# A hybrid decoder step on one core: the gate products of a mixture-of-experts expert run ahead of its up products, over four column groups, and expert 0's down products run behind expert 1's up products

## The reference, cut to what matters

```
def run_block(args):
    idx_b, e = args
    xb = xpad[idx_b]
    hb = jax.nn.silu(xb @ w_gate[e]) * (xb @ w_up[e])
    return hb @ w_down[e]
```

## Time and profile before

| | us |
|---|---|
| median of 3 runs | 1528.69 (1527.49 to 1530.44) |
| the profiled execution's own time | 1532.22 |
| its span, first to last instruction | 1530.1 |

### The profile page before, as it was taken

One profiled execution on the slowest core, in us unless ns is written; L12 is line 12 of the kernel. 1 busy time (PEld: TensorE's weight loads), 2 busy tenths in 40 slices (PEclk: granted clock), 3 DMA queues, 4 the chain that ended last, 5 costly groups with the idle time before them and its releaser, 6 DMA issues.

```text
span 1530.1 us, 19858 instructions
## 1 busy us (share of the span) xinstructions
PE 1325.7 (87%) x8056; PEld 764.3 (50%) x8056; DVE 531.9 (35%) x1086; ACT 263.2 (17%) x688; POOL 87.0 (6%) x251
## 2 busy tenths in 40 slices
PE   7999999999999999899778777867877876877786
PEld 6667777765579996354333333332332342342232
DVE  5287767332564445414003103102202202202234
ACT  4452232262231112030000000000000000000003
POOL 7800000010010002000000000000000000000000
PEclk9999999999999999888888988998987988987988
DMA  9332332361359845999999999999999999999997
GB/s 222 114 111 64 102 111 60 106 171 38 130 182 360 327 155 197 398 429 427 429 425 431 426 431 426 430 427 430 427 430 426 430 427 430 429 428 427 428 424 309
DMA packets 117111, 481.00 MB, mean 314 GB/s; under 512 B 17969, under 2 KB 85877, under 8 KB 90341
## 3 DMA queue, kind: packets, MB, share of 16 engines
q1 hardware_dynamic: 115432, 475.71, 78.0%
q0 software_dynamic: 1328, 4.37, 1.0%
q10 hardware_dynamic: 288, 0.04, 0.0%
HBM read 470.03 MB, written 10.78 MB: 314 GB/s over the span
## 4 chain that ended last, share of the span: by engine, by line
PE 54%; DMA 40%; DVE 2%; issue 1%; SPq 1%; ACT 1%; POOLq 0%; POOL 0%; ACTq 0%; DVEq 0%
DMA arena<-in_w_up 40%; PE ps L2290 20%; PE ps L2595 12%; PE ps L2343 7%; PE ps L2653 2%; PE ps L2360 2%; PE ps L2428 1%; PE ps L2225 1%; PE ps L2160 1%; PE ps L2148 1%; PE ps L2627 1%; SPq L585 1%; PE ps L2504 1%; DMA arena<-in_x_prompt 1%; PE ps L2212 1%
## 5 line engine op out<-in xcount | busy, mean ns | idle before, releaser
L2595 PE MATMUL ps<-arena 128*32 128x512 f32 x2048 | 294.1, 725 | 136.1 <-DMA arena<-in_w_up 134.7
L2290 PE MATMUL ps<-arena 128*128 128x336 f32 (+1 forms) x1152 | 328.3, 442 | 0.0
L2290 PEld LDWEIGHTS ps<-arena 128*128 128x128 f32 x1152 | 215.3, 190 | 95.9 <-issue 3.7
L2595 PEld LDWEIGHTS ps<-arena 128*32 128x32 f32 x2048 | 79.8, 129 | 323.5 <-issue 321.0
L2653 PE MATMUL ps<-arena 128*32 128x512 f32 x1024 | 147.6, 727 | 19.0 <-DVE arena L1924 18.3
L1912 DVE COPY arena<-ps 128x512 f32<-128x512 f32 x31 | 21.4, 692 | 406.6 <-PE ps L2595 406.5
L2428 PE MATMUL ps<-arena 128*128 128x128 f32 (+1 forms) x672 | 125.7, 318 | 0.0
L2428 PEld LDWEIGHTS ps<-arena 128*128 128x128 f32 (+1 forms) x672 | 95.3, 196 | 47.2 <-issue 24.9
L1232 ACT ACTIVATE arena<-ps 128x128 f32<-128x128 f32 x32 | 8.9, 277 | 625.0 <-PE ps L2627 624.9
L2343 PE MATMUL ps<-arena 128*128 128x128 f32 x896 | 106.0, 278 | 0.0
L2343 PEld LDWEIGHTS ps<-arena 128*128 128x128 f32 x896 | 101.8, 192 | 5.4 <-issue 4.8
(11 more groups left out here) (433 smaller groups left out, 1055.1 us busy)
## 6 DMA issues: line engine op xcount, KB each, us to landing
arena<-in_w_down SPq DMA_DIRECT2D x59, 2048.0 KB, 23.1
arena<-in_w_gate SPq DMA_DIRECT2D x57, 2048.0 KB, 19.0
arena<-in_w_up SPq DMA_DIRECT2D x57, 2048.0 KB, 23.4
arena<-in_w_in SPq DMA_DIRECT2D x15, 2048.0 KB, 9.2
arena<-in_w_out SPq DMA_DIRECT2D x8, 2048.0 KB, 9.9
arena<-in_w_gate SPq DMA_DIRECT2D x14, 1024.0 KB, 11.6
arena<-in_w_up SPq DMA_DIRECT2D x14, 1024.0 KB, 13.3
arena<-in_w_down SPq DMA_DIRECT2D x10, 1024.0 KB, 11.9
```

Source lines behind the costliest of these rows:

```text
L2290: mm = te.matmul(o, w, x, start=(k == 0), stop=(k == kt - 1))
L2595: mm = te.matmul(ps[CAP * x:CAP * x + CAP, 0, :], (xT0 if start else xt)[:, 4 * q + at, CAP * i:CAP * i + CAP], (next_second[up] if late a ...
```

## The change

It does four things.

1. An expert's pieces 0 to 3 are its gate weights and 4 to 7 its up weights. TensorE runs eight steps `s_` of one piece each: four of gate products, then four of up products, all over the four column groups.
2. The turn becomes two (`turn_half`): the gate half after step 3, the up half after step 7, each with its own DVE copy of the bank before it and 4 products against 32 columns of `fold`. Silu follows the gate half; the multiplication follows the up half.
3. A transfer of two pieces waits for two steps of the last expert, wherever it stands; the first six of expert 1 are single pieces. Expert 0's down products (`down(0, 0, False)`) stand behind expert 1's up products.
4. In expert 31 the parts of `add_back_third` stand ahead of steps 0, 2 and 4, and `take_rows` ahead of step 6 behind a wait for Silu. ACT takes Silu after the square of row group 1; DVE copies the gate sums between its fourth and fifth `add_part`.

The diff, cut to its core:

```diff
             sp.wait_ge(piece_loaded[3], 16)
-            sp.dma_start(next_second[1], A["w_up"][0, 1]...[:, 2048:4096])
+            sp.dma_start(next_second[1], A["w_gate"][0, 1]...[:, 6144:8192])
...
-            expert_weights(1, 1, [0, 2, 4, 6, 5, 7], True)
-            sp.wait_ge(piece_loaded[1], 32)
-            sp.wait_ge(piece_loaded[3], 32)
-            expert_weights(2, 1, [1, 3], True)
-            expert_weights(2, 2, [0, 2], True)
-            expert_weights(2, 2, [4, 5, 6, 7])
+            expert_weights(1, 0, [(0, 1), (1, 1), (4, 1), (5, 1), (6, 1), (7, 1)])
+            sp.wait_ge(piece_loaded[2], 32)
+            expert_weights(2, 0, [(2, 2)])
+            expert_weights(2, 8, [(0, 2), (4, 2), (6, 2)])
...
-            expert_weights(2, 1, [8, 9, 10, 11])
+            expert_weights(2, 8, [(8, 2), (10, 2)])
...
             expert(m_last, 2, None, False, True)
             load_table(ACT.Sqrt)
-            for t in range(2):
-                token_square(t)
-                token_root(t)
-            token_square(2)
+            token_square(0)
+            token_root(0)
+            token_square(1)
             load_table(ACT.Silu)
             expert(m_last, 3, None, True)
             load_table(ACT.Sqrt)
+            token_root(1)
+            token_square(2)
             token_root(2)
...
+                if not start:
+                    dve.wait_ge(weights_used, used + 4)
+                    ve.tensor_copy(GUs, ps[:, 0, :]).then_inc(gu_copied, 1)
...
+            def turn_half(n, i, up):
+
+                pe.wait_ge(gu_copied, 2 * n + 1 + up)
+                if up:
+                    pe.wait_ge(silu_ready, n + 1)
+                for k in range(4):
+                    at = 256 * (i % 2) + 4 * CAP * up + CAP * k
+                    mm = te.matmul(ps[:, 1, at:at + CAP], (hsel if isinstance(n, int) and n == 0 and not up else GUs)[:, k:HID:4],
+                                   fold[:, 0:CAP], start=True, stop=True)
+                mm.then_inc(gu_turned, 1)
...
-                for q in range(4):
+                for s_ in range(8):
+                    q, up = s_ % 4, s_ // 4
...
+                    if last and s_ in (0, 2, 4):
+                        add_back_third(m, s_)
+                        add_back_third(m, s_ + 1)
+                    if last and s_ == 6:
+                        pe.wait_ge(silu_ready, n + 1)
                         take_rows(m)
...
+                    wait_piece(n, s_, last)
+                    for x in range(4):
+                        mm = te.matmul(ps[CAP * x:CAP * x + CAP, 0, :], (xT0 if start else xt)[:, 4 * q + x, CAP * i:CAP * i + CAP],
+                                       (next_second[q - 2] if late and s_ in (2, 3) else wpiece[s_])[:, HID * x:HID * x + HID],
+                                       start=(q == 0), stop=(q == 3))
+                    mm.then_inc(weights_used, 1)
...
+                    if s_ == 3:
+                        turn_half(n, i, 0)
+                if late:
+                    down(0, 0, False)
+                turn_half(n, i, 1)
```

More of the change, by code:

```diff
@@ new lines, in expert_weights @@
+            def expert_weights(e, base, pieces):
+                for j, c in pieces:
+                    name, at = ("w_gate", "w_up", "w_down")[j // 4], j % 4
+                    if base is None and j < 8:
+                        sp.dma_start(arena[:, 2048 * j:2048 * (j + 1)].rearrange("p (x n) -> p x n", x=4),
+                                     A[name][0, e].rearrange("(x b p) n -> p b x n", x=4, b=4)[:, at])\
+                            .then_inc(piece_loaded[j], 16)
+                        continue
+                    if base is not None:
+                        sp.wait_ge(weights_used, base + j + c)
+                    rows = A[name][0].rearrange("e (p k) n -> e p (k n)", p=128)
+                    sp.dma_start(arena[:, 2048 * j:2048 * (j + c)],
+                                 rows[bass.ds(e, 1), :, 2048 * at:2048 * (at + c)].rearrange("e p n -> (e p) n"))\
@@ L1230, in expert @@
                     act.wait_ge(small_done, 1)
[L1231 to L1232 removed]
+                act.wait_ge(gu_turned, 2 * n + 1)
+                sc.activation(Hs, gate_up(i)[:, 0], ACT.Silu).then_inc(silu_ready, 1)
                 if last:
@@ L2551, in spread_gains, with wait_piece, down @@
                               start=True, stop=True).then_inc(gains_spread, 1)
+            LOADED = {(0, j): 16 for j in (0, 1, 2, 3, 4, 5, 6, 7, 8, 10, 11)}
+            LOADED.update({(1, j): 16 if j == 9 else 32 for j in range(12)})
+            LOADED.update({(2, j): 48 for j in range(0, 12, 2)})
+            LAST_LOADED = {5: 48, 7: 48, 9: 32, 11: 48}
+            def wait_piece(n, j, last):
+                if isinstance(n, int) and n < 3:
+                    if (n, j) in LOADED:
+                        pe.wait_ge(piece_loaded[j], LOADED[n, j])
+                elif j % 2 == 0:
+                    pe.wait_ge(piece_loaded[j], 16 * (n + 1))
+                elif last and j in LAST_LOADED:
+                    pe.wait_ge(piece_loaded[j], LAST_LOADED[j])
+            def turn_half(n, i, up):
[7 more added lines that the diff above has]
+                mm.then_inc(gu_turned, 1)
+            def down(n, i, last):
+                late = isinstance(n, int) and n == 1
+                pe.wait_ge(hid_ready, n + 1)
+                for k in range(4):
+                    wait_piece(n, 8 + k, last)
+                    for x in range(4):
+                        mm = te.matmul(ps[CAP * x:CAP * x + CAP, 6 + i % 2, :], HT[:, k, :],
+                                       (next_down[k] if late else wpiece[8 + k])[:, 512 * x:512 * x + 512],
+                                       start=(k == 0), stop=(k == 3))
+                    mm.then_inc(weights_used, 1)
             def expert(m, i, inputs, turned=None, over=False, ending=False):
@@ L2570, in expert @@
                     pe.wait_ge(xT_b, 2 * rows + 2)
-                for q in range(4):
-                    if start:
+                for s_ in range(8):
+                    q, up = s_ % 4, s_ // 4
+                    if start and not up:
                         pe.wait_ge(x0_ready, q + 1)
[L2574 to L2581, removed]
-                        take_rows(m)
[L2583 to L2601, removed]
@@ new lines, in expert @@
+                    if s_ % 2 == 0 and inputs is not None:
+                        if first and (i, s_ // 2) in GATHER_FIRST:
+                            gather(inputs, GATHER_FIRST[i, s_ // 2], None)
+                        elif not first and (i, s_ // 2) in GATHER_AT:
+                            gather(inputs, GATHER_AT[i, s_ // 2], m)
+                    if last and s_ in (0, 2, 4):
[3 more added lines that the diff above has]
+                        pe.wait_ge(silu_ready, n + 1)
+                        take_rows(m)
@@ L2602, in expert @@
+                    mm.then_inc(weights_used, 1)
+                    if start and s_ == 0:
                         turn_picked(1)
```

112 lines of the change are left out of this document (39 added, 73 removed).

## The result

The changed kernel takes 1538.97 us (median of 6 runs, 1535.29 to 1541.82), the kernel before 1529.53 us beside it (6 runs): 9.4 us more, a ratio of 1.006 with a 95% interval of 1.0045 to 1.0075. The profiled execution took 1541.36 us, its span is 1539.6.

A forecast was written before the change was run, and what follows sets the result against it. DMA transfers were taken to bound the kernel from 700 to 1490 us. Stream 2.5 us plus tail 7.0 us made 9.5 us over the 1528.69 us median, so 1538.2 us, range 1531.5 to 1547.

The forecast's parts named there:

- The start: First transfers around 610 to 635 us: stream about 0.5 us earlier, bounds 1.8 earlier and 1.5 later.
- Expert 0's down products moved: Experts 1 and 2: expert 1 starts near 627.7, expert 2 at 653.5 to 655.4, taken as 654, instead of 651.15.
- Round 0 becomes tight: Experts 2 and 3: expert 4's transfers released late behind turns and gathers, new gaps of 1 to 7 us, taken as 3.
- The stream term: Whole weight stream: 3 us of round 0 gaps less 0.5 us gained at the start, 2.5 us later.
- The tail, expert 30: Expert 30 after its landing: fewer instructions before add-backs offset one more turn, nothing in sum.
- 16 instructions instead of 32 (1.8 us less): Expert 30, before the first add-backs: half the instructions to do, saving 1.8 us.
- The tail, expert 31: Expert 31: TensorE waits 4.3 us for Silu at take_rows; end 7.0 us later, bounds 5.0 to 7.8.
- The table load: Before expert 31's Silu: Silu starts 1.41 us after the load; the skill's further 1.38 us drain left out.
- C: Rounds: PE becomes the bound, needing 29.5 to 30.2 us per expert against 29.4; near 1550 us, chance 0.11.
- the 3.3 of the sum: PE in each expert: 3.3 us of new work, giving 28.4 of 29.4 us.
- B: Tail only: gathers find full clock and the stream has no new round 0 gaps; near 1534.7 us, chance 0.22.
- D: Faster or same: Silu done before TensorE asks, by 1508.9; 1526.9 us, chance 0.06 faster, 0.06 for a draw.

The follow-up runs named there:

- the variant with Silu early: Changed kernel with ACT taking expert 31's Silu right after the square of row group 0, ahead of group 0's root and group 1's square: 1535.16 us, ratio 1.0026.
- the third turn: Changed kernel with the four products of each gate turn issued twice in rounds 1 to 6: 1539.76 us, ratio 1.0061.

## Why the prediction was right, point by point

The forecast of 1538.2 us and the measured 1538.97 agree, and so does the sum of 9.5 against 9.4. Inside it, two terms were off, expert 30 by 2.1 us and expert 31 by as much the other way, and cancelled. The mechanism was right; that the number is this close is luck.

- *The start.* Forecast 0.5 us ahead, measured 0.7 by the bytes up to 640 us. The gap at 633.53 shrank and a gap at 615 to 619 came, as described.
- *Expert 0's down products moved.* Forecast start of expert 2: 654, from 653.5 to 655.4; it was 652.83, under the range: expert 1 started at 627.23, and the moved down products ran at full clock (3.62 us) and hid the copy of the up sums.
- *Round 0 becomes tight.* Forecast release of the up pairs 696.4 to 699.1, of the down pairs 707.2 to 713.5, gaps of 3 us. Measured 698.95, 709.90 and 2.9 us. Here too two errors cancelled: expert 3 started at 682.12, 1.7 us ahead of the forecast, and its first 16 up instructions took 3.6 us at low clock where the sum had 1.9. The stream term of 2.5 us was 2.4 in this pair of profiles; over the other landings, single pairs give 2.3 to 5.6. With the gathers moved the gaps are gone, so it is these queues and nothing later.
- *The tail, expert 30.* Forecast: nothing in sum. Measured: 2.1 us shorter. The term "16 instructions instead of 32 (1.8 us less)" was mis-sized. The 32 took 5.34 us as part of them ran at 1.2 GHz after the wait for weights; in the changed kernel the first pair took that on, earlier and beside the stream, and the 16 after the landing ran in 1.92 us, 3.4 us less. That is how the clock fell in this execution; in three of the variants the 16 took 2.6 to 3.1 us.
- *The tail, expert 31.* Forecast 7.0, bounds 5.0 to 7.8; measured 9.1, beyond the bound. The mechanism was right: wait 4.5 us (4.3), Silu's end at 1513.58 (1513.2). I had priced take_rows at full clock (1.2 us, it took 2.0), taken the middle for steps 6 and 7 (it was 3.41, near the upper end) and left L2540 at its old 3.88 (it took 4.49). These three make the 2.1 us. In windows of 1 us the granted clock was 0.50 from 1512 to 1518, during and behind the 4.5 us of idle, 1.00 from 1519 to 1522, and 0.50 again from 1523 to 1525, behind the up turn and in the picking. The second fall does not need the idle: without it, in the variant with Silu early, the picking still took 4.06 us. The sizes are of one execution: in the second profile of the same kernel the wait was 2.99 us, and expert 31 took 36.1 us up to the end of its down products instead of 33.2.
- *The table load.* Silu started 1.40 us after it (1513.32 against 1511.92, L1223 and L968 in ACT's timeline). The instruction ahead of the load ended at 1511.90. The further 1.38 us of drain that the Trainium skill gives (ScalarE: Activation LUTs, "What ACT_TABLE_LOAD costs") is not there; the measurement decides.
- *The rivals.* C is excluded by the DMA share and by the third turn: 2.0 us more per expert went in without a gap, where my sum had left 1.0. The new work was 2.5 us of busy time per expert (603.6 against 543.5 over 700 us, for 23.8 experts), which with the copies is the 3.3 of the sum, so its other terms were too large, by 1.0 us or more. B did not come about: the gaps opened. D's condition, Silu before 1508.9, was met only by the edited order of ACT's program (1506.4), and even then the time came to 1.0026 of the kernel before.

## What to carry to other kernels

Where transfers bind a loop, as here with a DMA share of 1.01 before and after, finer release of buffers buys nothing inside it. It can pay only at the two ends, and there each step of the new order must be followed through every engine's program: here a Silu that stood behind a root and a square of another part of the work held up TensorE for 4.5 us, and moving it was worth 5 to 7 us of the 9 to 11. Work that releases nothing (gathers) belongs behind the work that releases buffers, while a stream has no margin; here that closed the gaps, though the timed gain stayed inside the intervals. And a stage in a profile is to be compared from its own start: what an execution's clock gave or took ahead of it is not the edit's.

## What had not been expected

The same kernel's tail differs from run to run by where TensorE's clock falls: in two profiles of the changed kernel the same 32 instructions took 3.64 us at 2.4 GHz or 6.30 with most of them at 1.2 GHz, and across the variants 16 add-back products took 7.13 or, once, 14.02 us. That the number of slow products differs between runs of one kernel is also what the Trainium skill says (TensorE: Matmul & The Clock Gate, "Part 1: The HAM clock gate (the "warmup" mystery)"); the two profiles of the changed kernel agree, with 2.7 us between them. It makes gains of 1 or 2 us in such a tail hard to time: landings 4.5 us earlier showed as medians 0.9 and 2.7 us lower.
